# A hybrid layer's output projection: weights and delta-rule rows prepared in the mixers, and the halves of its contraction run one after the other

## The chip, the cores and the metric

The kernel runs on one core of a Trainium2 chip. A core has TensorE (PE, matmuls), VectorE (DVE), ScalarE (ACT), GpSimd (POOL) and SyncE (SP, which here issues nearly all DMAs), each with its own instruction stream; they meet through semaphores. The metric is device time in microseconds (us), the median of several runs. Everything is float32.

## What is computed

One block over 1024 tokens of width 1024: two mixers, an output projection with a residual, a mixture of 64 experts, a gated embedding, a last norm. What matters here:

```python
h = rms_norm(x, ln_mix); proj = h @ w_in           # q, k, v, z, b, a of the delta rule; q, k, v of attention
# delta rule: 4 heads of 128, by chunk, state S: o = (q*exp(gc)) @ S + qk @ v_new;  S = S*exp(g) + k' @ v_new
gdn_out = rms_norm(o, gdn_norm_w) * silu(z)        # per head of 128 -> 512 columns
# stick-breaking attention: 8 heads of 64, weights from a running product over the keys
sb_out = rms_norm(attention, sb_norm_w)            # per head of 64  -> 512 columns
x = x + concat([gdn_out, sb_out]) @ w_out          # the output projection
x = x + moe(rms_norm(x, ln_moe))                   # router, top 2 of 64 experts
x = x + sigmoid(rms_norm(x) @ w_ple_gate) * (p @ w_ple_proj); return rms_norm(x, ln_final)
```

## The kernel before

Stages run one after the other, each a block of five streams that ends where all engines meet: `stage_front`, `stage_mixers`, `stage_output_projection`, routing, experts, per-layer embedding. Tokens are cut into `NT = 8` tiles (chunks) of 128.

**Front.** TensorE projects 20 column tiles (L253), each 128 channels for all tokens. After four of them (`ct` 12 to 15) it makes two Gram matrices each (`gram`, L276), for chunks 2i and 2i+1; `gram(c)` waits until VectorE has used Gram c-2 (`triangle`, L475). VectorE reaches `triangle(c-2)` only after the decays of chunk c: difference (L486, L488), ScalarE's exponential (L387), product with `r_k` (L490), two products (L492, L493). ScalarE comes to that exponential after it has copied the column tile (L377) and, for every chunk, made `egr` (L385), which GpSimd multiplies into `row_q` (L527).

**Mixers.** Eight bodies, written out for every engine as `both(body, e)`: body i does attention head i (12 strips of up to 512 keys, 15 steps) with chunk i of the delta rule in nine `pieces` between them. A strip goes TensorE logits (L629), ScalarE two sigmoids (L748, L749), VectorE scan (L808), GpSimd weights (L871), TensorE transposes two steps later (L640), weighted sum (L651). Pieces: `y1`, `qk`, `z1`, `vt_kt`, `y2`, `z2` (a blocked triangular inverse in `X`, `XT`, `Y`), `ks`, `vn`, `ods` (result and new state `St`). GpSimd makes `qe` = q times `row_q` at strip 1; `ods` does `qe`·`St` and `QKT`·`VN` into one PSUM tile `GB`, and ScalarE copies it to `mx` (L770). `mx` holds, per tile of tokens, 512 columns of the delta rule and 512 of attention. Attention's column is written only when its head is done, so those halves are complete with the last body's copy (L788).

**Output projection.** SyncE issues x and z of two tiles, 12 small loads of `nw`, `w_o` (4 MB), router weights, `ln_row`, then 8 MB of expert weights (`load_gate_up` twice). VectorE waits for `nw` and `w_o`, scales `w_o` by `nw` in eight instructions (L1062), then waits for the router's loads. Per tile: squares (ScalarE, L1025, L1026), sums by head (VectorE, L1068, L1069), a power (GpSimd, L1003), three products into `m_sb` (L1074, L1076, L1080; the last with z), eight transposes (L1126), a copy to `mT` (L1030), projection in two halves of the output columns (L1131), sum with x (L1086), row norm (L1037, L1008, L1010, L1093), transposes (L1139), router product (L1147). TensorE's order for tile t is: wait for the sum of tile t-1 (the accumulator `p_x` is single), half 0, transposes of h of tile t-1, transposes of mixed tile t+1, half 1, router of t-1.

## Time and profile before

| | us |
|---|---|
| timed runs, median (lowest, highest) | 1755.6 (1753.77, 1755.68) |
| profiled execution, its own time | 1750.28 |
| its span, first to last instruction | 1748.5 |
| TensorE busy in the span | 1465.7 (84%) |
| VectorE, ScalarE, GpSimd busy | 503.0, 374.6, 278.9 |

The span is the sum of its stages, since all engines meet between them: front to about 469, mixers 473 to 771, output projection 771 to 973, routing and the start of the experts to 1013, experts to about 1560, embedding to the end. So what counts in a stage is what its last engine waits for. Within a stage, a timeline row gives the start, the length, and in brackets how long the engine had been idle and what released it. The granted TensorE clock is given as a share: 1.00 is 2.4 GHz, 0.5 is 1.2 GHz.

### The profile page before, as it was taken

The numbers are of one execution on the slowest core, as the hardware profiler recorded it, in microseconds if no ns is written. First come the engines' busy times: TensorE is split into PE (matmuls) and PEld (weight loads), VectorE is DVE, ScalarE is ACT, GpSimd is POOL, SyncE is SP. The second block draws the span as 40 slices with busy tenths as digits, with TensorE's granted clock in tenths as the row PEclk, the third lists the DMA queues.
The fourth block names the chain that finished last, engine by engine and source line by source line (L and its number), as shares of the span: only waits on it lengthen the run. The fifth ranks groups of instructions, "written<-read, shape, count | busy, mean of one in ns | idle before, by whom it ended". The sixth has DMA issues, their size and how long they took to land. (4 is left out here: it accounts for less than half of the span.)

```text
span 1748.5 us, 17418 instructions
## 1 busy us (share of the span) xinstructions
PE 1465.7 (84%) x6018; PEld 786.2 (45%) x6018; DVE 503.0 (29%) x654; ACT 374.6 (21%) x666; POOL 278.9 (16%) x386
## 2 busy tenths in 40 slices
PE   7999998799899999965889377777787787848997
PEld 4557744344477778742455332222232322314443
DVE  4222034214035555533221411111111111112332
ACT  2221222100135565531221001000100100022221
POOL 1000002100124444421110111111111111100110
PEclk9999998889969999987999589898998989878999
DMA  5211057324002111136111249999999999961220
GB/s 185 72 61 49 1 183 197 92 81 113 1 1 61 30 30 30 30 112 262 60 60 42 109 181 420 389 406 404 408 415 395 397 402 397 399 271 71 79 78 36
DMA packets 106386, 306.41 MB, mean 175 GB/s; under 512 B 22368, under 2 KB 60912, under 8 KB 80368
## 3 DMA queue, kind: packets, MB, share of 16 engines
q1 hardware_dynamic: 96848, 289.16, 44.1%
q0 software_dynamic: 9504, 16.80, 2.6%
q8 instruction: 20, 0.33, 0.1%
q14 instruction: 14, 0.11, 0.0%
HBM read 283.85 MB, written 39.90 MB: 185 GB/s over the span
## 5 line engine op out<-in xcount | busy, mean ns | idle before, releaser
L1463 PE MATMUL pe_gu<-w_gu,xT 128*64 128x512 f32 x1024 | 273.2, 695 | 105.3 <-DMA w_gu<-in_w_expert_up 101.8
L253 PE MATMUL ps<-hT,gst 128*128 128x512 f32 x640 | 281.8, 600 | 2.7 <-DVE hT L410 2.7
L1463 PEld LDWEIGHTS pe_gu<-w_gu,xT 128*64 128x64 f32 x1024 | 83.7, 158 | 272.9 <-issue 271.2
L253 PEld LDWEIGHTS ps<-hT,gst 128*128 128x128 f32 x640 | 122.3, 193 | 151.8 <-issue 150.3
L808 DVE TENSOR_TENSOR_SCAN Pm<-rem,Pm 128x128 f32<-128x128 f32 (+3 forms) x96 | 114.4, 1192 | 115.1 <-ACT brk L749 115.1
L1556 DVE TENSOR_TENSOR hs<-sg,pe_gu 128x256 f32<-128x256 f32 x32 | 13.5, 421 | 378.7 <-ACT sg L1527 378.7
L1131 PE MATMUL p_x<-w_o,mT 128*128 128x512 f32 x256 | 119.0, 620 | 2.4 <-DVE mx L1086 1.3
L1481 PE MATMUL pe_y<-w_d,hTe 128*64 128x512 f32 x512 | 115.4, 592 | 1.1 <-DVE ys L1561 1.1
L1784 PE MATMUL f_pg<-w_gu,f_xT 128*128 128x512 f32 x256 | 114.7, 602 | 1.1 <-ACT f_xT L1702 1.1
L871 POOL TENSOR_TENSOR wt<-brk,Pm 128x128 f32<-128x128 f32 (+3 forms) x96 | 86.0, 896 | 176.1 <-DVE Pm L808 176.1
L267 PE MATMUL psk<-w_tok,hT 128*128 128x260 f32 (+1 forms) x384 | 111.7, 453 | 0.0
L1419 POOL DMA_INDIRECT y_d<-ys,row_at x32 | 32.9, 1028 | 435.6 <-DVE ys L1561 402.9
L629 PE MATMUL LB<-qk_st 64*128 64x128 f32 (+3 forms) x192 | 93.3, 568 | 4.2 <-POOL identb L861 4.2
L267 PEld LDWEIGHTS psk<-w_tok,hT 128*128 128x128 f32 x384 | 72.8, 190 | 38.0 <-issue 30.6
L1131 PEld LDWEIGHTS p_x<-w_o,mT 128*128 128x128 f32 x256 | 50.0, 201 | 60.9 <-issue 57.2
L651 PE MATMUL OB<-v_sb,wT 128*128 x576 | 77.2, 274 | 0.0
L1784 PEld LDWEIGHTS f_pg<-w_gu,f_xT 128*128 128x128 f32 x256 | 48.9, 194 | 60.3 <-issue 58.8
L651 PEld LDWEIGHTS OB<-v_sb,wT 128*128 128x128 f32 x576 | 74.9, 199 | 0.0
L1481 PEld LDWEIGHTS pe_y<-w_d,hTe 128*64 128x64 f32 x512 | 37.7, 137 | 72.8 <-issue 72.8
L1527 ACT ACT_TABLE_LOAD x16 | 20.5, 1283 | 231.6 <-PE pe_gu L1463 231.6
L748 ACT ACTIVATE rem<-LB 128x128 f32<-128x128 f32 (+3 forms) x96 | 47.2, 491 | 73.4 <-PE LB L632 34.6
L1561 DVE COPY ys<-pe_y 128x1024 f32<-128x1024 f32 x32 | 39.2, 1225 | 66.8 <-PE pe_y L1481 66.8
(269 smaller groups left out, 1538.1 us busy)
## 6 DMA issues: line engine op xcount, KB each, us to landing
w_gu<-in_w_expert_gate SPq DMA_DIRECT2D x64, 1024.0 KB
w_gu<-in_w_expert_up SPq DMA_DIRECT2D x64, 1024.0 KB
w_d<-in_w_expert_down SPq DMA_DIRECT2D x64, 1024.0 KB
gst<-in_w_in SPq DMA_DIRECT2D x20, 512.0 KB, 4.3
y_sb<-y_d SPq DMA_DIRECT2D x8, 1024.0 KB, 5.3
qkv_d<-y_sb SPq DMA_DIRECT2D x12, 512.0 KB, 2.6
qk_st<-rows_d SPq DMA_DIRECT2D x8, 768.0 KB, 7.5
gst<-qkv_d SPq DMA_DIRECT2D x8, 768.0 KB, 6.0
```

The lines of the kernel that those rows point to most:

```text
L253: last = pe.matmul(ps[s][:, c], w_ct[:, s, k, :], hT[:, k, c], start=k == 0, stop=k == KT - 1)
L267: last = pe.matmul(psk[:, bank, 0:n], hT[:, k, t * P:(t + 1) * P], w_tok[:, k, c0:c0 + n], start=k == 0, stop=k == KT - 1)
L629: last = pe.matmul(LB[k % 2][:, 0:c1 - c0], qk_st[:, s, 0, t * P:(t + 1) * P], qk_st[:, s, 1, c0:c1], start=True, stop=not diag)
L651: last = pe.matmul(OB[:, t, :], wT[:, k % 2, b * P:(b + 1) * P], v_sb[:, c0 // P + b, ds(i * SD, SD)], start=first and b == 0, stop=c0 == ...
L748: act.activation(rem[:, k % 2, 0:n], LB[k % 2][:, 0:n], ACT.Sigmoid, scale=-SD ** -0.5)
L808: dve.tensor_tensor_scan(out[:, ::-1], rem[:, k % 2, 0:n][:, ::-1], rem[:, k % 2, 0:n][:, ::-1], Pm[:, t % 2, o + c1:o + c1 + 1], ALU.mult ...
L871: pool.tensor_tensor(wt[:, k % 3, 0:n], brk[:, k % 2, 0:n], Pm[:, t % 2, o + c0 + 1:o + c1 + 1], ALU.mult).then_inc(w_done, 1)
L1131: last = pe.matmul(p_x[:, half, :], mT[:, s, k, :], w_o[:, k, half * 512:half * 512 + 512], start=k == 0, stop=k == KT - 1)
L1463: last = pe.matmul(p_gu[e * CAP:(e + 1) * CAP, :], xT[:, s, k, e * CAP:(e + 1) * CAP], wv[:, e, :, k, :], start=k == 0, stop=k == KT - 1)
L1481: last = pe.matmul(p_y[e * CAP:(e + 1) * CAP, h * 512:(h + 1) * 512], hT[:, c, e * CAP:(e + 1) * CAP], w_d[:, s, e, c, h * 512:(h + 1) * 5 ...
L1561: dve.tensor_copy(ys[:, s], p_y[:]).then_inc(ys_ok, 1)
L1784: last = pe.matmul(p_g[:, c], xT[:, s, k, :], w_g[:, k, c], start=k == 0, stop=k == KT - 1)
```

## The change

- **Front:** `egr` and `row_q` and their semaphore are gone; one more 32-column product, `col_q`, holds the same factor per token.
- **Mixers, delta rule:** the transposes of `X` move from `y1` to the next piece, now `xq`. q·`St` (unscaled) moves to `ks`, into `GB`; `ods` makes the state product first and `QKT`·`VN` second, into `GC`. VectorE scales `GB` by `col_q` into `mx` (four instructions) and adds `GC`.
- **Mixers, preparation:** SyncE loads z, `nw`, `w_o`, router weights and `ln_row` at the stage's start. VectorE scales `w_o` (now with k over its partitions in the other order, so that k 0 to 3 belong to the delta rule) in body 1, one eighth in front of each of eight pieces. Chunk i-1's rows are squared (ScalarE, `xq`), summed (VectorE, `z1`), raised (GpSimd, strip 6), normed and gated in place (VectorE, `y2`) in body i; the last chunk's in the projection (`gated_last`). ScalarE's, VectorE's and GpSimd's bodies 0 and 1 stand outside their loops.
- **Projection:** only attention's half is squared, summed and normed per tile, in place. TensorE transposes and projects the delta rule's half of the contraction (`turn_g`, `project(s, 0)`, both output halves) and then attention's (`turn_s`, `project(s, HK)`); its eight steps are written out.
- **Memory:** `hT` of the front and `w_o` share one buffer, `wide`.

```diff
-                    act.wait_ge(row_in[c % 2], 16 * (c // 2 + 1))
-                    if c >= 2:
-                        act.wait_ge(rq_done, c - 1)
-                    act.activation(egr[:, c % 2].rearrange("p h i -> p (h i)"), row_b[:, c % 2, 0, :], ACT.Exp).then_inc(egr_done, 1)
                     act.wait_ge(diff_done, c + 1)
                     act.activation(dec[:, c % 2], dec[:, c % 2], ACT.Exp).then_inc(exp_done, 1)
...
+                link(dve.tensor_tensor(col_q[:], egc[:], cols[:, 1, :], ALU.mult))
...
-                    pool.wait_ge(egr_done, c + 1)
-                    pool.wait_ge(row_in[s], 16 * (c // 2 + 1))
-                    pool.tensor_tensor(row_q[:, hs], egr[:, s], row_b[:, s, 1, :].rearrange("p (h i) -> p h i", h=GH), ALU.mult).then_inc(rq_done, 1)
                     pool.wait_ge(mat_done, c + 1)
...
+                load_z(0, 0)
...
+                sp.dma_start(nw[:, 0:1], A["gdn_norm_w"][0].rearrange("(p a) -> p a", a=1)).then_inc(nw_in, 16)
+                for r in range(P // SD):
+                    sp.dma_start(nw[r * SD:(r + 1) * SD, 1:2], A["sb_norm_w"][0].rearrange("(p a) -> p a", a=1)).then_inc(nw_in, 16)
+                sp.dma_start(w_o[:], A["w_out"][0].rearrange("(k p) c -> p k c", p=P)).then_inc(wo_in, 16)
+                sp.dma_start(w_r[:, :, 0:NG], A["w_router_group"][0].rearrange("(p k) c -> p k c", k=KT)).then_inc(small_in, 16)
+                sp.dma_start(w_r[:, :, NG:NG + NE], A["w_router_expert"][0].rearrange("(p k) c -> p k c", k=KT)).then_inc(small_in, 16)
...
                         load(i + 2, s)
+                        sp.wait_ge(nm_ok, i + 1)
+                        load_z(i + 2, s)
...
+                    if piece == "xq":
                         pe.wait_ge(chunk_in[s], j * 16 + 16)
                         pe.wait_ge(O_ok, i + 1)
+                        for h in range(GH):
+                            last = pe.transpose(GC[:, h, :], X[:, h, :], ident[:])
+                        last.then_inc(xt_done, 1)
...
+                        if n > 1:
+                            for h in range(GH):
...
+                        for h in range(GH):
+                            pe.matmul(GB[:, h, :], hd(q, h), St[:, h, :], start=True, stop=True)
...
-                        pe.wait_ge(qe_ok, i + 1)
                         pe.wait_ge(VN_ok, i + 1)
-                        for h in range(GH):
-                            pe.matmul(GB[:, h, :], qe[:, h, :], St[:, h, :], start=True, stop=False)
-                            last = pe.matmul(GB[:, h, :], QKT[:, h, :], VN[:, h, :], start=False, stop=True)
-                        last.then_inc(o_done, 1)
                         for h in range(GH):
                             last = pe.matmul(GA[:, h, :], kd[:, h, :], VN[:, h, :], start=True, stop=True)
                         last.then_inc(ds_done, 1)
+                        for h in range(GH):
+                            last = pe.matmul(GC[:, h, :], QKT[:, h, :], VN[:, h, :], start=True, stop=True)
...
+                    if piece == "xq" and not first:
+                        act.wait_ge(O_ok, i + 1)
+                        act.wait_ge(nss_ok, i)
+                        act.activation(nsq[:], mx[:, ds(i - 1, 1), 0:GW].rearrange("p a n -> p (a n)"), ACT.Square).then_inc(nsq_ok, 1)
...
-                    elif piece == "ods":
-                        act.wait_ge(o_done, i + 1)
-                        act.activation(mx[:, ds(i, 1), 0:GW].rearrange("p a n -> p (a n)"), flat(GB), ACT.Copy).then_inc(O_ok, 1)
...
+                    if scale:
+                        k = pieces.index(piece)
+                        if k < KT:
+                            dve.wait_ge(wo_in, 16)
+                            dve.wait_ge(nw_in, 48)
+                            last = dve.tensor_scalar(w_o[:, k, :], w_o[:, k, :], nw[:, k // GH:k // GH + 1], None, ALU.mult)
+                            if k == KT - 1:
+                                last.then_inc(wo_ok, 1)
...
+                        if n == 1 and not first:
+                            dve.wait_ge(nsq_ok, i)
+                            dve.tensor_reduce(nss[:], nsq[:].rearrange("p (h n) -> p h n", h=GH), AX.X, ALU.add).then_inc(nss_ok, 1)
+                    elif piece == "y2" and not first:
+                        o = mx[:, ds(i - 1, 1), 0:GW]
+                        dve.wait_ge(nrs_ok, i)
+                        dve.sem_inc(passed, 1)
+                        dve.tensor_tensor(o.rearrange("p a (h n) -> p (a h) n", h=GH), o.rearrange("p a (h n) -> p (a h) n", h=GH),
+                                          nss[:].unsqueeze(2).to_broadcast([P, GH, GD]), ALU.mult).then_inc(nz_step, 1)
+                        dve.wait_ge(nz_step, i)
+                        dve.wait_ge(z_in[1 - s], j * 16 + 16 if s else j * 16)
+                        dve.tensor_tensor(o.rearrange("p a n -> p (a n)"), o.rearrange("p a n -> p (a n)"), z_sb[:, 1 - s], ALU.mult).then_inc(nm_ok, 1)
...
+                        for h in range(GH):
+                            o = mx[:, ds(i, 1), h * GD:(h + 1) * GD].rearrange("p a n -> p (a n)")
+                            c = col_q[:, ds(i * GH + h, 1)]
+                            dve.tensor_scalar(o, GB[:, h, :], c, None, ALU.mult).then_inc(o_step, 1)
+                        dve.wait_ge(o_done, i + 1)
+                        dve.wait_ge(o_step, (i + 1) * GH)
+                        o = mx[:, ds(i, 1), 0:GW].rearrange("p a n -> p (a n)")
+                        dve.tensor_tensor(o, o, GC[:].rearrange("p h n -> p (h n)"), ALU.add).then_inc(O_ok, 1)
...
+                        if k == 6 and not first:
+                            pool.wait_ge(nss_ok, i + 1)
+                            pool.sem_inc(passed, 1)
+                            pool.tensor_scalar(nss[:], nss[:], 1.0 / GD, EPS, ALU.mult, ALU.add).then_inc(nms_ok, 1)
+                            pool.wait_ge(nms_ok, i)
+                            pool.tensor_tensor(nss[:], nss[:], nhalf[:], ALU.pow).then_inc(nrs_ok, 1)
...
+                head_squares(0, 0, None)
+                copy_g(0, 0)
+                head_squares(1, 1, None)
+                act.activation(hsq[:, 0:GW], row(NT - 1, slice(0, GW)), ACT.Square).then_inc(gsq_ok, 1)
+                copy_s(0, 0)
+                act.wait_ge(gs_sum, 1)
...
-                for k in range(KT):
-                    last = dve.tensor_scalar(w_o[:, k, :], w_o[:, k, :], nw[:, k:k + 1], None, ALU.mult)
...
-                norm_mixed(0, 0, 0, None)
-                norm_mixed(1, 1, 0, None)
+                sum_heads(0, 0)
+                norm_heads(0, 0)
+                sum_heads(1, 1)
+                norm_heads(1, 1)
+                gated_last()
                 add_to_x(0, 0, 0)
...
+                def turn_g(t, first):
+                    if not first:
+                        pe.wait_ge(gT_ok, t)
+                    for k in range(HK):
+                        last = pe.transpose(p_m[:, k, :], row(t, slice(k * P, k * P + P)), ident[:])
+                    last.then_inc(gtr_done, 1)
...
-                    for k in range(KT):
-                        last = pe.transpose(p_m[:, k, :], m_sb[:, s, k::KT], ident[:])
-                    last.then_inc(mtr_done, 1)
...
+                def project(s, k0):
+                    for half in range(2):
+                        for k in range(k0, k0 + HK):
+                            last = pe.matmul(p_x[:, half, :], mT[:, s, k, :], w_o[:, k, half * 512:half * 512 + 512],
+                                             start=k == 0, stop=k == KT - 1)
+                    if k0:
                         last.then_inc(mm_done, 1)
...
-                    project(t, s, 0)
-                    if not first:
+                    project(s, 0)
+                    if first:
+                        turn_s(0, True)
+                    else:
                         h_transposes(t - 1, 1 - s)
                     if not last:
-                        mixed_transposes(t + 1, 1 - s, False)
-                    project(t, s, 1)
+                        if t == NT - 2:
+                            pe.wait_ge(g_ok, 1)
+                        turn_g(t + 1, False)
+                        turn_s(t + 1, False)
+                    pe.wait_ge(sT_ok, t + 1)
+                    project(s, HK)
                     if not first:
                         route(t - 1)
```

TensorE at the start of the projection. Before, with `p_m` the transposed tile, `p_x` the accumulator and `p_h` the transposed h:

```order
L1126 MATMUL p_m<-ident,m_sb 128x128 x8
L1131 MATMUL p_x<-w_o,mT 128x512 x8
L1126 MATMUL p_m<-ident,m_sb 128x128 x8
L1131 MATMUL p_x<-w_o,mT 128x512 x8
L907 UNCONDITIONAL_BRANCH
L907 ISA
L1153 REGISTER_ALU
L1131 MATMUL p_x<-w_o,mT 128x512 x8
L1139 MATMUL p_h<-ident,h_sb 128x128 x8
```

After, the same place:

```order
L1179 MATMUL p_m<-ident,mx 128x128 x4
L1193 MATMUL p_x<-wide,mT 128x512 x8
L1187 MATMUL p_m<-ident,mx 128x128 x4
L1179 MATMUL p_m<-ident,mx 128x128 x4
L1187 MATMUL p_m<-ident,mx 128x128 x4
L1193 MATMUL p_x<-wide,mT 128x512 x16
L1201 MATMUL p_h<-ident,h_sb 128x128 x8
```

Only four transposes, read from `mx`, now stand ahead of the first projection; attention's transposes of tile 0 (L1187) follow it.

VectorE in a body of the mixers, from the piece `z1` to the strip after `y2`. Before, with `Pm` the scan:

```order
L828 COPY_PREDICATED X<-masks,GB 128x512
L804 REGISTER_ALU
L808 SCALAR_TENSOR_TENSOR Pm<-rem,Pm 128x128
L804 REGISTER_ALU
L808 SCALAR_TENSOR_TENSOR Pm<-rem,Pm 128x512
L819 ISA
L819 TENSOR_TENSOR vb<-GC,beta 128x512
L821 REGISTER_ALU
L821 TENSOR_TENSOR kd<-GA,col_kd 128x512
L804 REGISTER_ALU
L808 SCALAR_TENSOR_TENSOR Pm<-rem,Pm 128x256
```

After, in body 1, with `wide` the weights that are scaled and `nss` the sums by head:

```order
L860 COPY_PREDICATED X<-masks,GB 128x512
L863 TENSOR_REDUCE nss<-nsq 128x4
L832 SCALAR_TENSOR_TENSOR Pm<-rem,Pm 128x128
L832 SCALAR_TENSOR_TENSOR Pm<-rem,Pm 128x512
L843 TENSOR_SCALAR wide<-wide,nw 128x1024
L851 TENSOR_TENSOR vb<-GC,beta 128x512
L853 TENSOR_TENSOR kd<-GA,col_kd 128x512
L832 SCALAR_TENSOR_TENSOR Pm<-rem,Pm 128x256
L843 TENSOR_SCALAR wide<-wide,nw 128x1024
L868 TENSOR_TENSOR mx<-mx,nss 128x512
L872 TENSOR_TENSOR mx<-mx,z_sb 128x512
```

A sum, two products and two eighths of the scaling stand between the same scans; one of these eighths is ahead of `kd`, which TensorE's `y2` waits for.

## Rows read from the trace of the kernel before

**Rows 1.** Windows view: engines' us busy (instructions), TensorE clock, DMA share, GB/s.

```profile
474.00:514.00 40.00, 39.29 (x141) 27.71 (x141) 12.63 (x15) 13.93 (x32) 9.16 (x12) 0.55 0.00 1
...
550.00:587.00 37.00, 36.92 (x248) 28.29 (x246) 21.89 (x26) 21.16 (x46) 15.46 (x17) 1.00 0.15 36
...
770.00:805.00 35.00, 2.34 (x12) 1.83 (x11) 8.56 (x13) 2.02 (x4) 2.80 (x4) 0.55 0.83 313
805.00:980.00 175.00, 149.41 (x504) 82.51 (x504) 48.16 (x77) 34.32 (x49) 25.59 (x42) 0.92 0.19 74
...
1012.00:1500.00 488.00, 385.32 (x1674) 145.28 (x1674) 80.89 (x87) 41.53 (x73) 69.14 (x113) 0.90 0.96 388
```

**Rows 2.** Timeline 761:812, end of mixers, start of projection: start, length, engine, line, [idle, releaser].

```profile
761.75 1.11 DVE L834 SCALAR_TENSOR_TENSOR Rr<-GA,coef,vb 128x128 f32<-128x128 f32 x4
...
770.53 0.60 ACT L788 ACTIVATE mx<-OB 128x512 f32 x1 [1.30 <-PE OB L651]
...
778.90 8.11 SPq L970 DMA_DIRECT2D w_r<-in_w_router_expert  x1
...
790.15 5.39 DVE L1062 TENSOR_SCALAR w_o<-w_o,nw 128x1024 f32<-128x1024 f32 x8 [21.26 <-DMA w_o<-in_w_out]
```

**Rows 3.** TensorE's timeline of the projection: tiles 0, 1 and 7.

```profile
802.75 1.94 PE L1126 MATMUL p_m<-ident,m_sb 128*128 128x128 f32 x8 [32.35 <-DVE m_sb L1080]
805.80 9.58 PE L1131 MATMUL p_x<-w_o,mT 128*128 128x512 f32 x16 [1.11 <-ACT mT L1030]
...
824.45 7.13 PE L1131 MATMUL p_x<-w_o,mT 128*128 128x512 f32 x16 [1.31 <-DVE mx L1086]
...
834.42 1.88 PE L1126 MATMUL p_m<-ident,m_sb 128*128 128x128 f32 x8 [1.96 <-DVE m_sb L1080]
836.09 8.02 PE L1131 MATMUL p_x<-w_o,mT 128*128 128x512 f32 x16
...
946.89 7.08 PE L1131 MATMUL p_x<-w_o,mT 128*128 128x512 f32 x16
953.81 1.05 PE L1139 MATMUL p_h<-ident,h_sb 128*128 128x128 f32 x8
...
961.57 1.90 PE L1147 MATMUL p_r<-w_r,hT 128*128 128x72 f32 x16
```

**Rows 4.** Timeline 812:850: tile 0 leaves, tile 2 is normed.

```profile
823.18 1.22 DVE L1086 TENSOR_TENSOR mx<-o_x,p_x 128x1024 f32<-128x1024 f32 x1 [10.13 <-PE p_x L1131]
...
826.14 0.55 POOL L1010 TENSOR_TENSOR hss<-hss,o_nh 128x1 f32<-128x1 f32 x1
...
826.72 1.28 DVE L1093 SCALAR_TENSOR_TENSOR h_sb<-mx,hss,ln_row 128x1024 f32<-128x1024 f32 x1 [2.32 <-POOL hss L1010]
...
829.94 2.28 POOL L1003 TENSOR_TENSOR mss<-mss,o_nh 128x12 f32<-128x12 f32 x1
...
832.47 0.69 DVE L1074 TENSOR_TENSOR m_sb<-mx,mss 128x512 f32<-128x512 f32 x1 [3.28 <-POOL mss L1003]
```

**Rows 5.** Timeline 317:330: a pair of chunks in the front.

```profile
318.87 0.62 ACT L385 ACTIVATE sq_sb<-qk_st 128x512 f32<-128x512 f32 x1
...
319.57 1.27 POOL L527 TENSOR_TENSOR row_q<-sq_sb,qk_st 128x512 f32<-128x512 f32 x1 [18.41 <-ACT sq_sb L385]
...
320.04 1.35 DVE L490 TENSOR_TENSOR sq_sb<-sq_sb,r_k 128x512 f32<-128x512 f32 x1 [16.77 <-ACT sq_sb L387]
...
323.45 2.04 PE L276 MATMUL psk<-gst 128*128 128x128 f32 x8 [5.55 <-DVE decay_kk L475]
...
325.43 0.97 DVE L490 TENSOR_TENSOR sq_sb<-sq_sb,r_k 128x512 f32<-128x512 f32 x1 [0.69 <-ACT sq_sb L387]
```

**Rows 6.** Timeline 595:622: a body of the mixers.

```profile
608.44 0.68 DVE L821 TENSOR_TENSOR kd<-GA,col_kd 128x512 f32<-128x512 f32 x1
...
609.22 1.13 PE L680 MATMUL GA<-X,LT 128*128 128x128 f32 x8
```

**Rows 7.** Waits view of 514:770: us in total, times, longest.

```profile
DVE Pm L808 <- ACT brk L749: 89.3, 70, 4.0
```

More of the change, by code:

```diff
@@ L785, in body @@
                         for p in pieces_at(2 * k + 1):
-                            delta(p, i)
+                            delta(p, i, first)
                     act.wait_ge(pv_done, i * NS + (NS + 2))
                     act.activation(mx[:, :, ds(i * SD + GW, SD)], OB[:], ACT.Copy).then_inc(at_done, 1)
-                both(body, act)
+                body(0, 0, 0, True)
+                body(0, 1, 1)
+                with act.Fori(0, NT // 2 - 1) as j:
+                    body(j + 1, 0, 2 * j + 2)
+                    body(j + 1, 1, 2 * j + 3)
             @block.vector
@@ L847, in body @@
                         for p in pieces_at(2 * k) + pieces_at(2 * k + 1):
-                            delta(p, j, s, i)
-                both(body, dve)
+                            delta(p, j, s, i, first, scale)
+                body(0, 0, 0, first=True)
+                body(0, 1, 1, scale=True)
+                with dve.Fori(0, NT // 2 - 1) as j:
+                    body(j + 1, 0, 2 * j + 2)
+                    body(j + 1, 1, 2 * j + 3)
             @block.gpsimd
@@ L1163, in _ @@
                 pe.wait_ge(small_in, 80)
-                mixed_transposes(0, 0, True)
-                tiles_skewed(pe, step)
+                turn_g(0, True)
+                for t in range(NT):
+                    step(t, t % 2, t // 2, t == 0, t == NT - 1)
                 h_transposes(NT - 1, 1)
```

232 lines of the change are left out of this document (116 added, 116 removed).

## The prediction

> **What bounds the kernel now.** First the windows view [rows 1]. Between 770 and 805 TensorE works 2.34 us of 35 at a clock of 0.55 while DMA moves 313 GB/s: a stage that waits for its own loads. In the projection (805 to 980) it works 149.4 of 175, with no other engine over 28%. In the mixers it works 36.92 of 37 at full clock: TensorE bounds them, and work added elsewhere is free until it makes TensorE wait. The experts (1012 to 1500) run at a DMA share of 0.96: they move with the end of routing and give nothing back, as all but the first loads are released there by TensorE's progress.
>
> Then the timeline at the seam [rows 2]. The last mixer copy ends at 771.13. VectorE sits 21.26 us until w_o lands, scales it for 5.39, and waits for the router's loads; GpSimd's power and three products follow, and the first transposes start at 802.75, after 32.35 us of idle TensorE [rows 3]. Then its timeline in the steady state [rows 3]: each step with a mixed tile to turn has a wait like that of 834.42 (1.96 us for m_sb; six such, 1.89 to 2.01), and in some steps the clock falls after it, so that the half at 836.09 takes 8.02 us where the one at 946.89 takes 7.08. The chain behind that wait [rows 4]: sum done at 824.40, squares, power, norm of h to 828.00, sums by head, a power over 12 columns (2.28 us), three products of 0.69; the transposes start 10.0 us after the sum, but TensorE is back from half 0 and the h transposes after 8.0.
>
> **Part 1: the start of the projection.** w_o, nw and the router's loads are gone from it. I time the first step with the same pieces. From 771.4: four transposes are half of the 1.05 at 953.81 [rows 3], a copy of 512 columns 0.60 (as at 770.53 [rows 2]), 0.2 per hand-over: the first matmul at about 773.1. The delta half of tile 0 is 16 instructions (the trace shows each float32 matmul twice), as one half before: 953.81 - 946.89 = 6.9, to 780.0. Beside it attention's half is prepared: square 0.6, sum 0.7, power, product 0.69. The power over 8 columns is not in the trace; 1 column took 0.55 and 12 took 2.28 [rows 4], so it lies between, and I take 1.65, on the line through both. That has tile 0 ready at 776.0 and tile 1 at 779.4, both ahead of 780.0. The last chunk's norm and gate (about 4 us of VectorE and GpSimd) end before 784, ahead of the sum. Then 12 transposes with one copy of 0.6 between them: 782.0; the attention half 6.9: 788.9; drain and sum (0.4 + 1.22 [rows 4]): 790.5. Tile 1's projection then starts at 790.5, where before it started at 824.45 [rows 3]: **34.0 us**. If the clock drops at the seam, the first half costs 9.58 instead of 7.03 (the row at 805.80 against the warm ones): 2.6 less. If it goes better, at most the 1.3 of waiting comes back. Bounds 30 to 35.
>
> What must be hidden: x of tiles 0 and 1 is issued first and has until 788.9. The 8 MB of expert weights now start at once; with x that is 9 MB, at the 388 GB/s of the experts' row [rows 1] 23 us, to about 795. x of tile 2 queues behind them and has until its sum at about 825. In the mixers SyncE spends 8.11 us on one router load [rows 2]; its next job, chunk 2, comes at the end of body 0, some 50 us after the start, and all loads have until body 1 or the next stage.
>
> **Part 2: the steady steps.** Of the chain of 10.0 us the second sum, two products and 0.6 of the power go (0.7 + 1.4 + 0.6 = 2.7), so attention's half of tile t+1 is ready 7.3 us after the sum, and TensorE comes to it after 6.9 + 1.05 + 0.5. The wait disappears with about 1 us to spare, and the drops of the clock with it. A step is then the last one, which had nothing to turn, plus eight transposes and a router product: (961.57 - 946.89) + 1.05 + 1.90 = 17.6 [rows 3]. What is late next is the sum with x: the next step waits for it, but the router product lies over it, as now. From step 1 to step 7 before: 946.89 - 824.45 = 122.4; after 6 x 17.6 = 105.8: **16.6 us**. Bounds: 0, if the wait stays, and 17.7, if the instructions overlap at their ends as in the trace.
>
> **Part 3: the front.** At the second, third and fourth pair of Gram matrices TensorE waits for VectorE, 5.5 and then 3.0 us; the group shows one pair of three alike. On that chain lies ScalarE's egr (0.62 at 318.87 [rows 5]). The product with r_k takes 1.35 when it starts inside GpSimd's row_q (319.57 for 1.27), and 0.97 when it starts near that one's end; a like product alone takes 0.69 [rows 4]. With egr and row_q gone: 0.62 + 0.66 + 0.28 = 1.5 per pair, three pairs: **4.5 us**. Bounds 2 (egr alone) and 5.5. What follows in the front is TensorE's own work. The 32-column product costs VectorE 0.1 to 0.2 between convolutions, under TensorE's projections.
>
> **Part 4: the mixers.** TensorE's instructions are the same in number. The four q products stand in ks instead of ods, which delays vn by 0.95 us and puts it behind R with more room. ScalarE gets a square for a copy (0.6 each). GpSimd loses qe (1.3) and gets a power of 4 columns, between 0.55 and 2.28; on the same line 1.0, with its scaling 1.2. VectorE gets per body four small scalings (1.11 for four like them [rows 2]), a sum with PSUM, a sum by head and two products (0.69 each): 3.9 us on top of 21.89 of 37 [rows 1]. The scalings and the addition stand in the last three steps, which have no scan. The other three stand between scans; over these bodies VectorE waited 70 times for ScalarE's sigmoids, 89.3 us in all [rows 7], 1.3 per scan and up to 4.0. So I cost them at nothing; cover gone, each 0.69 would count. One place has no cover: kd ends at 609.12 and TensorE's y2 starts at 609.22 [rows 6]. In body 1 an eighth of the scaling (5.39 / 8 = 0.67) stands ahead of kd: I take **1 us lost** for it. Bounds: 0, and 5.4 if all eight count.
>
> First a row, then a rule. The product of 1.35 against 0.97 in the front [rows 5] shows that VectorE stands still while GpSimd reads. By the Trainium skill (SBUF — State Buffer, Who interferes with whom) the two share one pair of ports, and a VectorE instruction with two SBUF inputs, or a single-input one in a two-port mode, holds off a GpSimd instruction; the trace agrees, with these numbers. That speaks for part 3 and against part 4, since the scaling of w_o and the norms now run beside GpSimd's weights; rival A is its result.
>
> **The sum.** 34.0 + 16.6 + 4.5 - 1 = 54.1. Against the profiled execution: span 1748.5 - 54.1 = 1694.4, its time, 1.8 longer, 1696.2. The median of the timed runs lies 5.3 above that execution (1755.6 against 1750.28); the forecast for it is 1755.6 - 54.1 = **1701.5**.
>
> **Rivals.**
> *A, VectorE and GpSimd hold each other off in the mixers.* For it: the row of 1.35, and kd without cover. Against: 1.3 us of slack per scan, and GpSimd's own wait for scans. If the eight scalings (5.4) and seven times the two products (9.7) all delayed weights that TensorE waits for, it costs 15 us: 1716. Of short waits up to that I expect the range 1706 to 1716.
> *B, the steady wait stays*, because the power over 8 columns is no shorter or the new copies in ScalarE's queue come late. Then part 2 is lost, in part or whole: up to 1718. Against it: even with 2.28 the half is ready 7.9 us after the sum, 0.5 early.
> *C, slower than before.* Mechanism: the new VectorE work makes TensorE wait once in every body, and the clock falls as in body 0, where the window 474 to 514 shows 0.55 over 40 us with TensorE busy 39.29 [rows 1]: in this stage a low clock did not come back while it worked on. A body takes about 35 us at full clock (the stage's 298 us are eight of them, the first one slow) and loses some 17 at half. It decides from the fourth body on (54 / 17 = 3.2); with six more cold bodies 1701.5 + 102 = 1804. Against: the window 550 to 587 is at 1.00 [rows 1], with margins that the parts above keep.
> *D, better:* the low clock of body 0 ends earlier. No row tells why it lasts as long as it does, and the moved transposes may shift its end; half of its 36 us is up to 17: 1685 to 1695.
> *E, nothing of it:* the expert stage takes the gain back, at 1755. Against: its weights for the first pass are loaded during the projection, which stays long enough for 8 MB, and everything later hangs on TensorE.
>
> **Chances and range.** Forecast (1695 to 1706) 0.63, A 0.14, B 0.12, C 0.03, D 0.06, E 0.02. The range goes from 1690 to 1718: it holds the forecast, nearly all of A and B, and the half of D. A measurement of this kernel can tell about 0.2% (3.5 us) from no change. Faster 0.95, same 0.02, slower 0.03.
>
> **What would show it.** Right: the first projection matmul within 2 us of the last mixer copy; no wait of TensorE for normed rows between steps, steps 17.4 to 17.7 us apart; waits at the Gram matrices of about 4.3 and 2.7 instead of 5.5 and 3.0; bodies 35 us apart with a gap under 1 us in body 1. Wrong: TensorE waiting for kd, R or the transposed weights in bodies 2 to 7, a clock under 1.00 there, or the sum of tile 2 waiting for x.

## The result, and the profile after

The changed kernel takes 1688.9 us (median of four executions, 1686.6 to 1690.9) against 1754.8 (1753.8 to 1755.7): a ratio of 0.962, 95% interval 0.961 to 0.964. That is 65.9 us less where 54.1 were forecast, and 1.1 us below the range. (The forecast starts from 1755.6, the median of the three runs of before then at hand; from 1754.8 it would be 1700.7.) The profiled executions, 1750.28 and 1688.82, differ by 61.5; their spans by 61.4. Cut at the same instructions, the spans give:

| stretch | before | after | gain | forecast |
|---|---|---|---|---|
| start to the mixers' first logits | 473.24 | 472.37 | 0.9 | 4.5 |
| first body of the mixers | 52.3 | 39.2 | 13.2 | 0 |
| the seven others | 244.8 | 245.4 | -0.5 | -1 |
| end of the mixers to tile 1's projection | 54.05 | 21.45 | 32.6 | 34.0 |
| tile 1 to tile 7 | 122.44 | 104.19 | 18.25 | 16.6 |
| tile 7 to the experts | 66.2 | 66.2 | 0 | 0 |
| experts to the end | 735.4 | 738.3 | -2.9 | 0 |

First the windows view of after, cut at these places; its columns are those of [rows 1].

```profile
472.30:480.00 7.70, 6.55 (x27) 5.23 (x27) 1.34 (x2) 2.30 (x6) 2.69 (x4) 0.57 0.76 257
480.00:512.00 32.00, 31.56 (x214) 24.41 (x214) 19.65 (x26) 16.43 (x36) 11.50 (x12) 1.00 0.34 115
512.00:756.90 244.90, 242.58 (x1651) 188.46 (x1650) 164.59 (x225) 135.44 (x301) 100.81 (x110) 1.00 0.14 38
756.90:778.35 21.45, 17.83 (x48) 8.28 (x49) 5.87 (x8) 4.58 (x9) 4.99 (x7) 0.92 0.90 366
778.35:882.50 104.15, 104.15 (x384) 58.19 (x384) 23.45 (x29) 21.99 (x36) 15.55 (x24) 1.00 0.20 76
```

The same view of before, of its first body:

```profile
473.20:481.00 7.80, 7.04 (x27) 5.46 (x27) 1.24 (x2) 2.30 (x6) 3.47 (x5) 0.50 0.00 1
481.00:511.00 30.00, 30.00 (x104) 21.34 (x104) 10.36 (x12) 10.05 (x23) 6.49 (x8) 0.51 0.00 1
511.00:525.80 14.80, 14.80 (x110) 12.34 (x108) 6.94 (x9) 7.02 (x14) 6.32 (x5) 1.00 0.01 2
```

Here lies the miss. In before the clock stays at its lower level (0.50, 1.2 GHz) for 38 us, in 30 of which TensorE is busy all the time (104 matmuls); in after it is back at the full level by 480, with 214 matmuls in the next 32 us. The last row of after's table, six steps of the projection, has no idle time and no low clock: the waits like that of 1.96 us [rows 3] are gone.

TensorE's timeline of after at the seam and in one steady step (start, length, engine, line, operation, [idle, releaser]); these rows answer [rows 3]:

```profile
758.09 0.63 PE L1179 MATMUL p_m<-ident,mx 128*128 128x128 f32 x4 [1.20 <-PEq L602]
759.41 8.83 PE L1193 MATMUL p_x<-wide,mT 128*128 128x512 f32 x16 [0.69 <-ACT mT L1077]
...
778.35 7.10 PE L1193 MATMUL p_x<-wide,mT 128*128 128x512 f32 x16 [1.40 <-DVE mx L1125]
785.29 1.05 PE L1201 MATMUL p_h<-ident,h_sb 128*128 128x128 f32 x8
786.18 0.60 PE L1179 MATMUL p_m<-ident,mx 128*128 128x128 f32 x4
786.62 0.60 PE L1187 MATMUL p_m<-ident,mx 128*128 128x128 f32 x4
787.06 7.03 PE L1193 MATMUL p_x<-wide,mT 128*128 128x512 f32 x16
793.92 1.90 PE L1209 MATMUL p_r<-w_r,hT 128*128 128x72 f32 x16
795.72 7.11 PE L1193 MATMUL p_x<-wide,mT 128*128 128x512 f32 x16
```

The idle 32.35 us of [rows 3] have become 1.20 and 0.69. From 778.35 to 795.72 a step takes 17.37 us. The two halves of p_m (L1179 the delta half, L1187 attention's) follow each other without a gap. The chain that had been late [rows 4], in after's timeline one step on:

```profile
800.50 1.65 POOL L1047 TENSOR_TENSOR mss<-mss,o_nh 128x8 f32<-128x8 f32 x1
802.30 0.69 DVE L1120 TENSOR_TENSOR mx<-mx,mss 128x512 f32 x1 [2.28 <-POOL mss L1047]
...
803.99 0.60 PE L1187 MATMUL p_m<-ident,mx 128*128 128x128 f32 x4
```

The power over 8 columns takes 1.65 us, as interpolated; the product ends at 802.99, 1.0 us ahead of the transposes that read it.

Two smaller differences lie outside the change's terms. At the start after loses 2.9 us by its first Gram matrices (its first loads land 0.4 later, and transposes and products run at the lower clock for longer). That belongs to the execution: the first logits came at 470.0 to 473.8 (mean 471.7) in seven traces of after and of variants that leave everything ahead of them alone, and at 473.2 to 479.1 (mean 476.6) in seven of before and its variants, less what these add. The profiled execution of before was the earliest of its kind: the means are 4.9 us apart where the two profiled executions are 0.9 apart, which can account for nearly all of the 4.4 us by which the medians are farther apart than the profiled executions. In the experts TensorE waits 105.7 us for w_gu instead of 101.8. That too is mostly the execution: from the experts' first transposes to the end eight traces of before and its variants took 732.9 to 738.2 us, ten of after and its variants 734.4 to 738.8, with means of 735.6 and 737.1.

### The profile page after: what moved, and what is told of

It reads as the page before. It is cut to its first block and busy times, and to the rows that moved or that the text cites. A ratio compares the mean times of both kernels' runs of the same rounds, so it can differ in the third digit from the quotient of the medians.

```text
span 1687.1 us, 17290 instructions
## 1 busy us (share of the span) xinstructions
PE 1446.6 (86%) x6018; PEld 772.1 (46%) x6018; DVE 510.7 (30%) x695; ACT 361.8 (21%) x655; POOL 261.9 (16%) x379
## 5 line engine op out<-in xcount | busy, mean ns | idle before, releaser
L1532 PE MATMUL pe_gu<-w_gu,xT 128*64 128x512 f32 x1024 | 273.5, 695 | 109.1 <-DMA w_gu<-in_w_expert_up 105.7
L251 PE MATMUL ps<-wide,gst 128*128 128x512 f32 x640 | 284.7, 605 | 2.7 <-DVE wide L404 2.7
L251 PEld LDWEIGHTS ps<-wide,gst 128*128 128x128 f32 x640 | 123.4, 195 | 153.9 <-issue 152.1
L832 DVE TENSOR_TENSOR_SCAN Pm<-rem,Pm 128x128 f32<-128x128 f32 (+3 forms) x96 | 108.0, 1125 | 76.4 <-ACT brk L766 76.3
L1193 PE MATMUL p_x<-wide,mT 128*128 128x512 f32 x256 | 114.8, 602 | 2.1 <-DVE mx L1125 1.4
L265 PE MATMUL psk<-w_tok,wide 128*128 128x260 f32 (+1 forms) x384 | 111.7, 453 | 0.0
L642 PE MATMUL LB<-qk_st 64*128 64x128 f32 (+3 forms) x192 | 87.9, 538 | 3.8 <-POOL identb L918 3.8
L265 PEld LDWEIGHTS psk<-w_tok,wide 128*128 128x128 f32 x384 | 72.8, 190 | 38.0 <-issue 30.6
L1193 PEld LDWEIGHTS p_x<-wide,mT 128*128 128x128 f32 x256 | 47.9, 192 | 57.8 <-issue 56.9
L1630 DVE COPY ys<-pe_y 128x1024 f32<-128x1024 f32 x32 | 39.2, 1224 | 66.8 <-PE pe_y L1550 66.8
```

The lines of the kernel that those rows point to most:

```text
L251: last = pe.matmul(ps[s][:, c], w_ct[:, s, k, :], hT[:, k, c], start=k == 0, stop=k == KT - 1)
L265: last = pe.matmul(psk[:, bank, 0:n], hT[:, k, t * P:(t + 1) * P], w_tok[:, k, c0:c0 + n], start=k == 0, stop=k == KT - 1)
L642: last = pe.matmul(LB[k % 2][:, 0:c1 - c0], qk_st[:, s, 0, t * P:(t + 1) * P], qk_st[:, s, 1, c0:c1], start=True, stop=not diag)
L832: dve.tensor_tensor_scan(out[:, ::-1], rem[:, k % 2, 0:n][:, ::-1], rem[:, k % 2, 0:n][:, ::-1], Pm[:, t % 2, o + c1:o + c1 + 1], ALU.mult ...
L1193: last = pe.matmul(p_x[:, half, :], mT[:, s, k, :], w_o[:, k, half * 512:half * 512 + 512], start=k == 0, stop=k == KT - 1)
L1532: last = pe.matmul(p_gu[e * CAP:(e + 1) * CAP, :], xT[:, s, k, e * CAP:(e + 1) * CAP], wv[:, e, :, k, :], start=k == 0, stop=k == KT - 1)
```

## The experiments

**Which part ended the low clock?** Four kernels, of after and of before. The expectations weigh three theories: 'order' (the moved transposes end it), 'loads' (the new traffic does) and 'moment' (it hangs on when TensorE is idle).

The first (e1_xt_back) puts one piece of the order back:

```
 xq (TensorE):
     pe.wait_ge(O_ok, i + 1)
-    transposes of X into GC, xt_done
 y1:
+    pe.wait_ge(O_ok, i + 1)
     products LT x X
+    transposes of X into GC, xt_done
```

> The kernel after with one thing undone: the first transposes of X stand again in y1, right behind the first product, and not in xq (y1 now also waits for O_ok, because GC is read by the addition of the body before). The question is the first body of the mixers: in before it took 52.3 us with a granted clock of 0.51 for 37 us, in after 39.2 us with the clock back at 1.00 after 8 us. Theory 'order' (the place of these transposes ends the low clock): the first body takes about 52 us again, the time is about 1689 + 13 = 1702. Theories 'loads' (the DMA traffic of the new loads ends it) and 'moment' (the time at which TensorE's idle stretch falls ends it): the first body stays near 39 us and the time at 1689 to 1692, the wait for O_ok costing 0 to 0.4 us a body.

Measured: 1687.6 us (1684.4 to 1688.4), no slower than after. The first body took 41.8 us, the clock returning 13.8 us behind the first logits instead of 7.6. 'Order' fell in its strong form: in after the place of the transposes moved the end by 6 us, not by 30.

The second (e2_loads_late) holds the loads back until the first body is over:

```
+    sp.wait_ge(S_ok, 2); sp.wait_ge(log_done, NS)
     load_z(0, 0)
     ... the other loads of the mixers
```

> The kernel after with its mixer loads (z, nw, w_o, router, ln_row) issued only when the first body is over, so that the first body has no DMA traffic, as in before; all are still in time for body 1's end or cost body 1 a wait. Theory 'loads': the low clock of the first body lasts 37 us again, body 52 us, time about 1702. Theories 'order' and 'moment': first body near 39 us; body 1 waits for w_o, which lands some 12 us after its issue, at its first scaling: VectorE is held for up to 10 us and body 1 grows by up to that; time 1689 to 1699.

Measured: 1702.1 us (1695.2 to 1707.3). The first body stayed at 39.1 us with no load in it, so 'loads' fell. Body 1 grew to 59.5 us, though, by far more than expected. The waits view of TensorE over that body, and windows of it:

```profile
PE GB L713 <- DVE QKT L851: 12.2, 1, 12.2
```

```profile
511.00:520.00 9.00, 4.11 (x22) 2.22 (x20) 0.00 (x0) 2.99 (x8) 0.26 (x1) 0.92 0.92 338
520.00:530.00 10.00, 2.70 (x12) 2.64 (x12) 5.26 (x6) 1.28 (x3) 1.93 (x2) 0.50 0.74 229
530.00:550.00 20.00, 20.00 (x70) 14.34 (x70) 9.91 (x14) 7.08 (x17) 6.83 (x7) 0.50 0.24 66
```

VectorE waits for w_o ahead of QKT, TensorE for QKT, 12.2 us; and then it works for over 20 us without a pause at the lower clock. This is rival C's mechanism with a price: 22.8 us of body for a wait of 12.2. But the traced execution was the longest of the four (1707.3), and the shortest, 1695.2, is only 6.3 above after's median, so the price differs from one execution to the next. In after the loads cost no such wait, as they are issued a body ahead of their use.

The third (e3_before_xq) makes in before the opposite of the first edit (transposes of X and ScalarE's copy of them moved from y1 into qk):

> The kernel before with one thing of the change: the first transposes of X move from y1 into the piece qk, ahead of its products, ScalarE's copy with them. Theory 'order': the first body falls from 52.3 to about 39 us, time about 1755 - 13 = 1742. Theories 'loads' and 'moment': nothing, 1754 to 1756, unless the moment moves with it (it does not: the stage starts at the same time).

Measured: 1741.3 us (1736.6 to 1746.8), the first body 38.4 us. That is what 'order' said; but the fourth (e4_before_late), which changes no order at all, does the same:

```
+    for n in range(4):
+        pool.memset(pad[:, n], 0.0)
     pool.memset(negb[:], 0.0).then_inc(pool_step, 1)
```

> The kernel before with the start of the mixers put off: GpSimd clears four spare tiles of 512 columns ahead of the masks for which TensorE waits, about 4 x 0.45 = 1.8 us. Theory 'moment' (the length of the low clock hangs on when and how long TensorE is idle, not on what it then runs): the first body's cold stretch changes by several us against before's 37, to either side; if it falls to about 8 us as in after, time 1755 + 1.8 - 13 = 1744. Theories 'order' and 'loads': the first body stays at 52 us, time 1755 + 1.8 = 1757.

Measured: 1738.7 us (1736.0 to 1740.8), a ratio of 0.990 to before (0.988 to 0.992): work was added to the critical path, and 15 us gained. The windows of its first body:

```profile
479.00:483.70 4.70, 3.89 (x16) 3.18 (x16) 0.48 (x1) 1.04 (x3) 3.31 (x4) 0.50 0.00 0
483.70:516.60 32.90, 32.81 (x222) 25.38 (x221) 19.01 (x22) 18.03 (x39) 13.03 (x13) 1.00 0.01 1
```

TensorE runs the same instructions as in before; at the lower clock for 4.7 us instead of 38. So 'order' is not needed, but e3 leaves it some part: there TensorE's idle stretches are before's (4.14 and 0.71 us), only the order differs, and all five executions were short.

What differs at this place between before and after, besides the order, are these idle stretches. Before, then after:

```profile
473.24 0.79 PE L629 MATMUL LB<-qk_st 64*128 64x128 f32 x2 [4.15 <-POOL identb L861]
474.96 2.05 PE L680 MATMUL GA<-X,LT 128*128 128x128 f32 x8 [0.71 <-POOL LT L879]
```

```profile
472.37 0.48 PE L642 MATMUL LB<-qk_st 64*128 64x128 f32 x2 [3.78 <-POOL identb L918]
474.09 2.05 PE L696 MATMUL GA<-X,LT 128*128 128x128 f32 x8 [1.08 <-POOL LT L936]
```

The loads are not needed for the early end in after (e2), nor are the moved transposes (e1). Which part of the change brought it stays open.

**The terms of the sum.** Four kernels on after. The first (e5_warm) fills TensorE's idle time with throw-away products (512 columns, ident against v_sb): four ahead of the first logits, two ahead of the first y1, three at the end of the mixers, one in the projection.

> The kernel after with idle TensorE given throw-away products of 512 columns: four ahead of the first logits of the mixers (idle 3.8 us), two ahead of the first y1 (idle 1.1), three behind the last product of the mixers and one behind the first transposes of the projection (idle 1.2 and 0.7). Each takes 0.44 us at full clock. If the low clock at both places comes from this idle time: first body about 35 us instead of 39.2 (-4), first half of the projection 6.9 to 7.1 us instead of 8.8 (-1.7), time 1683 to 1684. If the clock has another cause: the same lengths as in after, time 1689 to 1691, the extra products costing up to 1.

Measured: 1687.6 us (1685.6 to 1690.2): no clear gain, though the clock did what was wanted: first body 36.8 us, first half 7.12. A throw-away product costs 0.92 us, not 0.44 (the trace shows each float32 matmul twice, which I had forgotten), so the fill ran past the idle time: it held the logits up by 1.6 us, and the projection's first transposes by 1.9 (3.07 us behind the mixers' last matmul instead of 1.19).

The second (e7_scale_late) takes the eight scalings out of body 1 and puts them at the projection's start:

```
-    body(0, 1, 1, scale=True)
+    body(0, 1, 1)
 projection, VectorE:
+    for k in range(KT): w_o[:, k, :] *= nw[:, k // GH]
     dve.wait_ge(small_in, 80)
```

> The kernel after with the eight scalings of w_o out of body 1 and at the start of the projection (the loads stay in the mixers). If the scalings are what makes body 1 longer than the six behind it (36.7 against 34.77): body 1 falls to about 34.8 (-1.8), and TensorE's first projection waits for 8 x 0.67 = 5.4 us of VectorE more, a little less as its idle 1.9 us cover some: +4 to +5.4, and TensorE idle longer may start at the low clock (up to +2). Time 1689 + 2 to 1689 + 6 = 1691 to 1695. It also tells what of the 32.6 us at the seam is the scaling's share. If body 1 has another reason for its length, it stays at 36.7.

Measured: 1692.4 us (1691.8 to 1694.8), 3.5 more. Body 1 fell from 36.69 to 34.84; TensorE's wait at the seam rose:

```profile
760.23 1.11 PE L1184 MATMUL p_m<-ident,mx 128*128 128x128 f32 x4 [6.57 <-DVE wide L1152]
```

6.57 instead of 1.20. So of the 32.6 us at the seam 5.4 are the scaling, and it costs 1.8 in the mixers.

The third (e8_egr_back) puts egr (ScalarE) and its product (GpSimd) back into the front, with a spare output:

> The kernel after with the exponential of the rows (ScalarE) and its product (GpSimd) put back into the front, the product going to a spare tile that nothing reads. If these two are what shortened the waits at the Gram matrices: TensorE's waits at the second, third and fourth pair go back from 4.4 and 2.7 us to 5.5 and 3.0, the stretch from the first of these matrices to the last transposes from 79.2 to about 83.6 us, time 1689 + 4.3 = 1693. If only the load of the other engines in general counts: half of that or less.

Measured: 1692.0 us (one execution). TensorE's timeline in this kernel, then in after:

```profile
325.89 2.04 PE L278 MATMUL psk<-gst 128*128 128x128 f32 x8 [5.55 <-DVE decay_kk L478]
330.91 2.04 PE L278 MATMUL psk<-gst 128*128 128x128 f32 x8 [2.98 <-DVE decay_kk L478]
```

```profile
323.24 2.05 PE L274 MATMUL psk<-gst 128*128 128x128 f32 x8 [4.37 <-DVE decay_kk L470]
327.97 2.05 PE L274 MATMUL psk<-gst 128*128 128x128 f32 x8 [2.69 <-DVE decay_kk L470]
```

The waits of before, 5.55 [rows 5] and 2.98, are back to 0.01 us. The difference is 1.2 + 0.3 a pair; before and after differ by 4.3 us from the first of these matrices to the last. The run puts both instructions back at once; what each is worth shows in after's VectorE:

```profile
320.48 0.69 DVE L485 TENSOR_TENSOR sq_sb<-sq_sb,r_k 128x512 f32<-128x512 f32 x1 [15.29 <-ACT sq_sb L381]
```

The product with r_k takes 0.69 where it took 1.35 and 0.97 [rows 5]: 0.66 and 0.28 us come from GpSimd's product. The other 0.5 of the 1.2 is ScalarE's egr, since the exponential behind it now starts 0.92 us after the copy of the column tile started (318.90 to 319.82) instead of 1.44 (317.95 to 319.39).

The fourth (e9_long_chain) lengthens the projection's chain on spare data to what it was:

```
+    dve.tensor_reduce(mss[:, s, SH:], ...)       second sum
     power over SH + GH = 12 columns, not 8
+    two products of 512 columns ahead of m_ok
```

> The kernel after with the chain behind the sum in the projection made as long as in before, on spare data: a second sum (0.7 us), the power over 12 columns instead of 8 (+0.63), two more products (1.4). The halves and the order of TensorE stay as in after. If the length of this chain is what made TensorE wait: it goes over by 2.7 - 1.0 (the margin between the end of the chain at 802.99 and TensorE's transposes at 803.99) = 1.7 us in each of six or seven steps, steps of 19.1 instead of 17.37, time 1689 + 10 to 1689 + 13, and some steps at a low clock, up to +6 more: 1699 to 1708. If the order (delta half first, halves of p_m) is what took the wait away: 1689 to 1691.

Measured: 1695.2 us (1694.8 to 1700.4), 6.3 more. Its waits view and its timeline:

```profile
PE p_m L1195 <- DVE gx L1127: 8.4, 7, 1.5
```

```profile
806.45 0.66 PE L1195 MATMUL p_m<-ident,mx 128*128 128x128 f32 x4 [1.20 <-DVE gx L1127]
806.94 7.03 PE L1201 MATMUL p_x<-wide,mT 128*128 128x512 f32 x16
815.60 7.11 PE L1201 MATMUL p_x<-wide,mT 128*128 128x512 f32 x16
```

The wait is back in every step; steps take 18.79 us instead of 17.37. Before's took 20.4. So the shorter chain is worth 1.4 of the 3.0 us a step. The rest can be read from before, where two steps went so:

```profile
845.73 7.10 PE L1131 MATMUL p_x<-w_o,mT 128*128 128x512 f32 x16
855.73 1.16 PE L1126 MATMUL p_m<-ident,m_sb 128*128 128x128 f32 x8 [2.01 <-DVE m_sb L1080]
856.72 7.03 PE L1131 MATMUL p_x<-w_o,mT 128*128 128x512 f32 x16
...
865.33 7.08 PE L1131 MATMUL p_x<-w_o,mT 128*128 128x512 f32 x16
...
875.19 1.71 PE L1126 MATMUL p_m<-ident,m_sb 128*128 128x128 f32 x8 [1.89 <-DVE m_sb L1080]
876.69 8.20 PE L1131 MATMUL p_x<-w_o,mT 128*128 128x512 f32 x16
...
886.50 7.11 PE L1131 MATMUL p_x<-w_o,mT 128*128 128x512 f32 x16
```

A step without a drop of the clock took 19.60 us, one with a drop 21.2, three of each: the clock is worth 0.8 a step on average, and no step of e9 has it. The last 0.8 is the wait, 1.20 here against 2.01. Counted from the start of the step's first half, TensorE is back after 8.44 us instead of 7.99, as the delta half's transposes (0.44) now stand ahead of the wait, and the chain ends after 9.64 instead of 10.00. Only the chain was varied by a run; the other two parts are read from the traces.

**How fine is the alignment?** Two throw-away products ahead of the first logits of before and one ahead of y1 (e10_before_warm) take the drop away altogether:

> The kernel before with two throw-away products of 512 columns ahead of the first logits of the mixers and one ahead of the first y1 (0.92 us each, in TensorE's idle 4.15 and 0.71 us). If the first body's long low clock is only what follows on this idle time: no drop, first body 34.9 to 35.5 us instead of 52.5, time 1755 - 17 = 1738 or a little under. If something in the body itself holds the clock down (its narrow or short products): the first body stays over 45 us, time over 1748.

Measured: 1738.3 us (1734.9 to 1741.8), first body 36.2, at full clock from its start. So the body's own instructions do not make the clock fall; the idle time ahead of them does.

Then the spare clears of e4, with one tile (e11) and with two (e14):

> The kernel before with one spare tile cleared ahead of the masks (0.45 us) where the run with four had 1.8 us and lost the long low clock. If the length of the low clock hangs on fine alignment between the idle stretch and what the chip looks at: any value from 4 to 38 us, time 1739 to 1756, and not necessarily between its neighbours'. If only a longer idle time cures it: it stays near 37 us at 0.45 us, time 1755.

> As the run with one cleared tile, with two (0.9 us). Alignment: the first body between 37 and 53 us, time 1739 to 1756, in no fixed order with the runs with 0, 1 and 4 tiles. Length of the idle time: between before (1755) and the run with four (1739), in order.

Measured: 1741.4 us (eight executions, 1735.0 to 1745.1) and 1742.1 (six, 1737.6 to 1742.5); first bodies 38.0 and 38.0. One clear costs 0.5 us and cures as well as four. Two more, with a tile of 128 columns (e17, some 0.15 us) and with eight tiles (e16, 3.7 us):

> The kernel before with one spare tile of 128 columns cleared ahead of the masks, so that the mixers begin 0.15 to 0.2 us later. If the 38 us of low clock hang on one exact alignment: first body 37.5 to 42 us, time 1738 to 1745. If a band of starts has it: first body 52.5, time 1754.

> The kernel before with eight spare tiles cleared, 3.7 us later. If the long low clock recurs at other alignments: first body over 45 us, time over 1752 (before plus 3.7 less a part of 14). If not: first body 37.5 to 42, time 1740 to 1745.

Measured, here each execution counts: with 0.15 us three of ten took 1740 to 1744 and seven 1751 to 1759; with 3.7 us three of five took 1740 to 1744 and two 1759 to 1761. The mean granted clock over the whole kernel was 0.918 to 0.920 in these six short executions and 0.910 to 0.914 in the nine long ones. Of 46 executions of before that ran beside the experiments one took 1739.3, all others 1747 or more. So the two lengths of the first body (52.3 and 38 us where they were traced) are two outcomes of the same program, and the means of the two groups lie 12.7 us (e17) and 17.2 us (e16) apart. The spare clears shift the odds, by the length of TensorE's idle stretch or by the moment at which it ends (no run separates the two), and so does the order of what TensorE then runs (e3). The profiled execution of e16 was of the long kind:

```profile
483.00:517.00 34.00, 33.29 (x113) 23.13 (x113) 9.84 (x12) 11.59 (x28) 8.62 (x11) 0.50 0.00 1
517.00:534.80 17.80, 17.80 (x124) 15.30 (x123) 8.71 (x11) 7.76 (x15) 7.18 (x6) 0.93 0.00 1
```

What decides it inside the chip stays open.

**The rest.** With the power alone back at 12 columns (e18_power_12):

> The kernel after with the power in the projection over 12 columns instead of 8 (0.63 us longer), nothing else. The margin between the end of the chain and TensorE's transposes is 1.0 us, so no wait is expected: steps of 17.37 us as in after, time 1689. If the margin is smaller than it looks: a wait of a few tenths per step, up to +3.

Measured: 1688.7 us (one execution), steps of 17.37 as in after and no wait between them. Of the margin of 1.0 us at least 0.63 is real.

e6_scale_behind, with each scaling behind the delta rule's piece instead of ahead of it (`delta(p, ...)` first, then `w_o[:, k, :] *= nw`):

> The kernel after with each scaling of w_o in body 1 behind the delta rule's piece instead of ahead of it, and nothing else. In the combined version body 1 took 35.23 us. Expected here: body 1 35.2 instead of 36.7, TensorE's wait for vb (1.2 us) and for R (0.6) gone, first body as in after (39), time 1689 - 1.5 = 1687.5.

Measured: 1686.1 us (1684.7 to 1690.0); body 1 35.26 us instead of 36.69. In after body 1 has these waits of TensorE:

```profile
PE GA L696 <- DVE vb L851: 1.2, 1, 1.2
PE GC L724 <- DVE Rr L878: 0.6, 1, 0.6
```

Both are gone: what TensorE waits for was queued behind a scaling that nobody waited for. The body is 1.4 us shorter in the trace; the medians, 1686.1 and 1688.9, overlap in their executions.

**A version that beats both** (e12_warm_behind): that order, and the fill cut to the idle time.

```
+    warm(2)      ahead of the first logits (2 x 0.92 us)
+    warm(1)      ahead of the first y1
+    warm(1)      behind the last product of the mixers
+    one product  behind the first transposes of the projection
```

> A version meant to beat both: the kernel after with throw-away products of TensorE only where it is idle (two ahead of the first logits, one ahead of the first y1, one behind the last product of the mixers, one behind the first transposes of the projection), and with each of the eight scalings of w_o in body 1 behind the delta rule's piece instead of ahead of it, so that it no longer delays vb, kd and R. Expected: first body 35 to 35.5 instead of 39.2 (-4), body 1 35 to 35.8 instead of 36.7 (-1 to -1.7), first half of the projection 7.1 instead of 8.8 (-1.7): 1689 - 7 = 1682, between 1680 and 1685. If a scaling behind a piece delays the next scan as much as one ahead delayed the piece, body 1 stays at 36.7 and the time is 1684.

Measured: 1680.3 us (five executions, 1675.3 to 1682.1), a ratio of 0.957 to before (0.954 to 0.960). Windows of the first two bodies and of the first half:

```profile
470.60:507.00 36.40, 35.69 (x239) 27.21 (x238) 20.98 (x28) 18.27 (x41) 14.25 (x16) 1.00 0.44 152
507.00:542.30 35.30, 34.81 (x238) 27.01 (x237) 28.21 (x39) 19.46 (x43) 16.82 (x16) 1.00 0.18 47
753.70:761.00 7.30, 7.30 (x21) 3.42 (x21) 2.58 (x4) 0.98 (x2) 4.00 (x6) 1.00 1.00 402
```

All three are at full clock. The first body is 36.5 us, 1.1 of it fill and 0.3 a wait for GpSimd.

## Why the prediction was right or wrong

**The step that failed** is the claim that the first body stays as it is. The sum left its low clock in, and rival D, which had it end early, got a chance of 0.06. D came true: 13.2 us, three quarters of the 17 that it allowed. With this term the sum is 54.1 + 13.2 = 67.3, against 65.9 measured. D's own guess at the cause, the moved transposes, was not borne out: with them back (e1) the body still took only 41.8 us. The argument ahead of it was not wrong, since no row told why the low clock lasted; but "no row tells why" was taken as a reason for it to stay. It should have been a reason for a wide chance, because the change moves what stands around the start of the body: before had this length in nearly every execution, and half a microsecond more of idle time ended it. Which part of the change ended it is not known, so that it went in every execution of after was luck as far as the forecast goes. With D at a half the range would have begun at 1685.

**Start of the projection**, 34.0 forecast, 32.6 measured. The first matmul came 1.8 us behind the last mixer copy (within 2, as said). The first half took 8.83 us, not 6.9, at a low clock: the 2.6 named for that, in part. The scaling's share is 5.4 (e7); the rest, the loads and the serial first step, was not split further.

**Steady steps**, 16.6 forecast, 18.25 measured, bounds 0 to 17.7. Steps of 17.37 fell just short of "17.4 to 17.7": instructions overlap at their ends more than the sum of lengths says, and six times 0.26 is the difference. The mechanism held: power 1.65, margin 1.0, and the long chain brings the wait back (e9). The clock's part, 0.8 us a step, went with the wait, as said.

**Front**, 4.5 forecast, 4.3 measured between the Gram matrices, shown by e8; the waits of 4.4 and 2.7 are those forecast (the last one of the third pair was 3.22). The two terms held as well: with GpSimd's product gone the product with r_k is shorter by 0.66 and 0.28, and egr is worth 0.5, not 0.62. The stretch as a whole gained only 0.9, for the start of the execution.

**Mixers**, 1 us lost forecast, 0.5 measured as the sum of 1.8 lost in body 1 and 1.2 won in the six behind it, which the forecast had not. I placed the loss at kd and y2; it was there (1.2 us for vb, which with kd is queued behind a scaling) and at R. VectorE's three operations between scans cost TensorE nothing in bodies 2 to 7 (34.77 us each, where before alternated between 34.9 and 35.05).

**Rivals.** A (VectorE and GpSimd hold each other off) is there but small: beside a scaling GpSimd's weights of 512 columns took 1.52 us, 0.43 more than the 1.09 of the last row, for 0.57 us side by side:

```profile
520.23 0.72 DVE L843 TENSOR_SCALAR wide<-wide,nw 128x1024 f32<-128x1024 f32 x1
520.38 1.52 POOL L928 TENSOR_TENSOR wt<-brk,Pm 128x512 f32<-128x512 f32 x1 [1.16 <-DVE Pm L832]
...
531.48 1.09 POOL L928 TENSOR_TENSOR wt<-brk,Pm 128x512 f32<-128x512 f32 x1 [3.15 <-DVE Pm L832]
```

It met slack in bodies 2 to 7, and in body 1 it costs little: e6 keeps all eight scalings in the body and takes 35.26 us where e7, without them, takes 34.84, which leaves 0.4 us for it. By the Trainium skill (SBUF — State Buffer, Who interferes with whom) a VectorE instruction in a two-port mode and a GpSimd instruction shut each other out for the whole instruction, whichever came first; the trace agrees as far as these numbers go. B did not come; C did not, but a price for it was seen (e2). Of E there is no clear sign: the experts' 2.9 us lie within what single executions differ by.

## What to carry to other kernels

A stretch at a low clock that the trace of before shows while TensorE is busy need not be a property of the stage (here it was not): where a change moves TensorE's idle stretches at all, give its whole length a real chance of going, and of coming. Filling short idle stretches of TensorE ahead of a dense stage with throw-away products took the low clock away in the traces of e5, e10 and e12, but measure their length first, since one product too many stands on the path (e5). And when optional work is put into an engine's queue, put it behind the piece that another engine waits for.

## What the runs showed that I had not expected

The same instructions ran 38 us at the lower clock with TensorE busy nearly throughout (before), or under 5 us (e4), and adding 0.5 us of waiting gained 12 us (e11). By the Trainium skill (TensorE: Matmul & The Clock Gate, Part 1 on the clock gate) being busy is what releases the lower clock; the 30 us with 104 matmuls and no pause at 0.51 do not fit that, nor do the 20 us in e2. Among the caveats of that part the Trainium skill mentions a gate seen stuck at a quarter of the clock for more than 50 us; here the level was a half, and whether it is the same no run here can tell.

The power on GpSimd takes 0.55 us over 1 column, 1.01 over 4 (bodies 2 to 7), 1.65 over 8 and 2.28 over 12: 0.16 a column and 0.4 to start.

A wait of 12.2 us in a body of 36.7 cost 22.8 us in the one trace of e2: behind a wait of TensorE the low clock can cost about as much again.
